# A prefetch hint for the branch that closes the loop over the experts, on three engines

## The reference, cut to what matters

```python
logits = h @ w_router + b_router
top_val, top_idx = lax.top_k(logits, TOP_K)          # TOP_K = 4 of 32
gates = softmax(top_val)
# for every expert e, on the rows xb that chose it:
gu = xb @ w_gu[e] + b_gu[e]                           # 1024 -> 2048
x_glu, x_lin = split(gu, 2)
act = min(x_glu, 7) * sigmoid(1.702 * min(x_glu, 7)) * (clip(x_lin, -7, 7) + 1)
out = (act @ w_down[e] + b_down[e]) * gate            # 1024 -> 1024
acc[tok] += out
```

## Time and profile before

| what | value |
|---|---|
| median of three runs | 1286.19 us |
| the profiled execution's own time | 1288.51 us |
| its span, first to last instruction | 1286.3 us |
| granted TensorE clock, mean | 0.949 of full speed |
| TensorE matmuls busy | 88% of the span |
| VectorE, ScalarE busy | 32%, 15% |
| traffic of the DMA queues | 454.88 MB, mean 354 GB/s |
| chain of work that ended last | TensorE 67%, DMA 20%, VectorE 4%, issue 4% |

### The profile page before, as it was taken

One profiled execution on the slowest core, in us unless ns is written; L12 is line 12 of the kernel. 1 busy time (PEld: TensorE's weight loads), 2 busy tenths in 40 slices (PEclk: granted clock), 3 DMA queues, 4 the chain that ended last, 5 costly groups with the idle time before them and its releaser, 6 DMA issues.

```text
span 1286.3 us, 20674 instructions
## 1 busy us (share of the span) xinstructions
PE 1132.5 (88%) x6676; PEld 496.9 (39%) x6677; DVE 417.8 (32%) x1283; ACT 195.4 (15%) x419; POOL 43.9 (3%) x27
## 2 busy tenths in 40 slices
PE   4999998967877788799999998999999989869997
PEld 0667664643332222244333443443333333214432
DVE  2133735342333323312522224223332233331233
ACT  2323242141100000001111011010111011001110
POOL 0141101010000000000000000000000000000000
PEclk9998999986998999899999989999999999989898
DMA  9963229622999999999999989989999999999992
GB/s 379 347 228 141 68 85 373 258 86 109 420 421 422 422 422 422 421 422 400 410 422 422 422 323 417 423 339 421 422 423 421 422 421 423 421 423 421 405 394 106
DMA packets 76882, 454.88 MB, mean 354 GB/s; under 512 B 9868, under 2 KB 14732, under 8 KB 24524
## 3 DMA queue, kind: packets, MB, share of 16 engines
q1 hardware_dynamic: 70304, 449.76, 85.8%
q10 hardware_dynamic: 6540, 4.60, 1.3%
HBM read 451.17 MB, written 3.17 MB: 353 GB/s over the span
## 4 chain that ended last, share of the span: by engine, by line
PE 67%; DMA 20%; DVE 4%; issue 4%; ACT 2%; SPq 2%; POOL 0%; DVEq 0%; ACTq 0%
PE psum L867 24%; DMA ring<-w_gu 16%; PE psum L904 14%; PE psum L567 6%; PE psum L923 4%; PE psum L836 3%; PE psum L776 3%; PE psum L576 2%; DMA ring<-w_down 2%; SPq L481 2%; DMA ring<-w_ada 2%; PE psum L531 1%; PE psum L844 1%; PE psum L860 1%; PE psum L878 1%
## 5 line engine op out<-in xcount | busy, mean ns | idle before, releaser
L867 PE MATMUL psum<-ring,work 128*32 128x512 f32 (+2 forms) x2048 | 432.5, 621 | 34.0 <-DMA ring<-w_gu 32.5
L867 PEld LDWEIGHTS psum<-ring,work 128*32 128x32 f32 (+2 forms) x2048 | 131.6, 133 | 286.1 <-issue 196.6
L904 PE MATMUL psum<-ring,work 128*32 128x256 f32 (+2 forms) x1504 | 219.5, 480 | 18.8 <-issue 10.4
L1619 DVE SCALAR_TENSOR_TENSOR x<-psum,tiny,x 128x256 f32<-128x256 f32 (+1 forms) x512 | 155.2, 377 | 213.7 <-PE psum L923 213.7
L1588 DVE TENSOR_SCALAR work<-csb 96x128 bf16<-96x128 f32 x64 | 15.4, 280 | 403.0 <-PE psum L867 402.0
L980 ACT ACTIVATE work<-psum 128x256 f32<-128x256 f32 (+6 forms) x207 | 88.5, 443 | 345.7 <-PE psum L904 220.7
L904 PEld LDWEIGHTS psum<-ring,work 128*32 128x32 f32 (+2 forms) x1504 | 87.7, 130 | 136.4 <-issue 109.6
L1236 ACT ACTIVATE work<-work 128x128 f32<-128x128 f32 (+2 forms) x64 | 25.0, 391 | 573.2 <-DVE work L1602 573.2
L567 PE MATMUL psum<-h,ring 128*128 128x320 f32 x320 | 91.3, 443 | 1.2 <-ACT h L1015 1.2
L923 PE MATMUL psum<-work 32*128 32x320 f32 (+2 forms) x512 | 83.1, 481 | 1.4 <-ACT work L980 1.1
L567 PEld LDWEIGHTS psum<-h,ring 128*128 128x128 f32 x320 | 62.0, 195 | 26.9 <-issue 1.6
(11 more groups left out here) (209 smaller groups left out, 615.8 us busy)
## 6 DMA issues: line engine op xcount, KB each, us to landing
ring<-w_gu SPq DMA_DIRECT2D x256, 1024.0 KB, 20.6
ring<-w_down SPq DMA_DIRECT2D x128, 1024.0 KB, 18.9
ring<-w_ada SPq DMA_DIRECT2D x12, 2048.0 KB, 9.3
ring<-w_in SPq DMA_DIRECT2D x7, 2048.0 KB, 29.9
ring<-w_out SPq DMA_DIRECT2D x2, 2048.0 KB, 11.5
x<-xT SPq DMA_DIRECT2D x1, 1280.0 KB, 6.0
yT<-x SPq DMA_DIRECT2D x2, 640.0 KB, 3.9
work<-b_exp ACTq DMA_DIRECT2D x3, 384.0 KB, 16.4
```

The source lines that it names most:

```text
L867: last = mm(o, xg[:, kk, 0:m], cols(ring[:, kk, :]), start=False, stop=kk == KD - 1)
L904: last = mm(o, actT[:, kk, 0:m], ring[:, GU_UNITS + kk // 2, c1_:c1_ + n], start=False, stop=kk == 7)
L1619: last = stt(x[:, f, cols], bank[SPREAD_BANKS[u]][:, cols], mod[:, 40 + f, sq_:sq_ + 1], x[:, f, cols], ALU.mult, ALU.add)
```

## The change

The loop over the experts 1 to 30 in `passes` asks for a prefetch hint for its own closing branch, on each of the three engines that run `passes`. It is the same loop otherwise; the engine is now named explicitly since the option belongs to the general form of the loop.

```diff
             start(0, 0, 0)
             expert(0, 0, 0, True, False)
             most = eng.value_load(cmaxi[0:1, 0:1], min_val=0, max_val=T)
-            with eng.Fori(1, NE - 1) as e:
+            with nc.Fori(1, NE - 1, engines=[eng.engine], hint_back_edge=True) as e:
                 expert(e, e, 0, False, False)
             expert(NE - 1, NE - 1, 0, False, True)
             finish(NE - 1, 0)
```

## The result

The changed kernel takes 1291.78 us in the median (14 runs, 1289.36 to 1295.95) and the kernel before, in the same comparison, 1287.87 us (14 runs). The ratio is 1.0030, 95% interval 1.0016 to 1.0045: slower by 2 to 6 us. The prediction said 1287.0 us and a range up to 1290.8, with 0.89 for a change within 0.3%. It started from 1286.19 us, the median of the first three runs of the kernel before; the median of fourteen lies 1.7 us higher.

What follows compares the result with a forecast made beforehand. Weight transfers were taken to set the pace mostly, TensorE at large experts and the tail. Nothing removed plus 0.8 us added to the 1286.19 us median gave 1287.0 us, range 1284.0 to 1290.8 us.

Steps and rivals of the forecast that it cites:

- What bounds the kernel, and the fetches: Experts' loop: transfers mostly set the pace, TensorE at large experts and the tail; no code fetched, so the hint removes 0 us.
- What the change adds: Head of each loop body: one instruction on three engines, 30 times, taken at 0.16 us each, between 36 ns and 0.30 us.
- 26.4: Sign to look for: TensorE's 14 open waits ahead of L860 grow from 24.2 to about 26.4 us in total.
- Where it lies: VectorE and ScalarE hide the instruction beside waits; TensorE's 14 open edges between bodies take it, 2.2 us, but most are absorbed.
- I count five: 5 x 0.16 = 0.8 us: TensorE's edges between bodies: about five, mainly by large experts, count in full at 0.16 us each, 0.8 us in all.
- 14 x 0.30 = 4.2 us: Upper bound of the cost: all 14 open TensorE edges count, each at a register load's 0.30 us.
- (a): Loop's closing branch: the hint is dropped or costs no time, 1286.2 us; chance 0.10.
- (b): TensorE's closing branch shortens from 208 to 76 ns, 1285 us, chance 0.03; or unseen fetches vanish, 1277.6 us, chance 0.03.
- The 76 ns: Lowest of 30 records of TensorE's closing branch, median 208 ns; taken as a hinted branch's length, saving at most 0.13 us per edge.
- (c): Loop's head is fetched again though present, throwing nothing out; 1288.8 us; chance 0.05.
- (d): TensorE's code between L836 and L904: the fetched head displaces a needed block, 1.6 to 3.9 us per iteration, 1300 to 1340 us; chance 0.07.

Runs made afterwards that it cites:

- e1_plain: Against the kernel before: the loop in the general form with the engine named, no hint, same instructions; ratio 1.0013 (0.9995 to 1.0032).
- e3_act_dve_hint: Against the kernel before: the hint on ScalarE and VectorE alone, none on TensorE; ratio 1.0004 (0.9985 to 1.0023).
- e9_load_mid: Against the kernel before: no hint, one more load of the expert's count in the middle of TensorE's loop body; ratio 1.0001 (0.9981 to 1.0022).
- e5_pe_load: Against the kernel before: no hint, one more load of the expert's count at the head of TensorE's loop body; ratio 1.0030 (1.0011 to 1.0050).
- e11_late_again: Against the kernel before, second run: the hint on TensorE alone, in the middle of the body instead of at its head; ratio 1.0006 (0.9983 to 1.0028).

## Why the prediction was wrong

**What bounds the kernel, and the fetches: right.** No instruction packet in the loop before or after. The hint has nothing to bring in: the body is on the engine after its first pass. The Trainium skill ("Runtime: NRT & Kernel Launch", Instruction fetch mechanics) has only two blocks held and a taken branch beyond them fetched anew, which could have made the hint a gain. Every profile here speaks against that rule for this loop: none of the fourteen has an instruction packet between 366 and 1236 us.

**What the change adds: right in kind and size.** One record per body and engine; 0.15 us at an open edge, with the longer branches in it, against the 0.16 us assumed. The open waits grew to 26.6 us where 26.4 was said; that this is so close is owed in part to the 0.48 us ahead of expert 28.

**Where it lies: right for two engines.** VectorE and ScalarE pay nothing that can be seen, although their branches doubled in length, which was not foreseen.

**The step that failed** is the sum: "I count five: 5 x 0.16 = 0.8 us". It took a delay at an edge to cost its own length where it counts and nothing where it doesn't. The measured cost is 3.9 us by the loop (942.6 us in the mean of the four profiles with TensorE's hint at the head, 938.7 in the three without any), and about 3 us of these lie in experts 10 to 17: 252.5 us before, 255.5 after. Taken apart in the changed kernel's profile, expert 16 has 1.8 us, 1.7 of it in matmuls at the lower clock, expert 17 has 0.8 with the clock at 0.94 for 0.97, and experts 10 and 15 with the edges behind them have 0.3 each; experts 11 to 14 are even. So 1.7 of the 3.9 us are the clock's at expert 16, a term that the sum did not have. The 0.8 us of expert 17 may be the clock's too, but that isn't shown: its clock is at 0.94 without any hint at the head in e1_plain, e3_act_dve_hint and e9_load_mid as well (53.08 to 53.12 us), and experts 10 to 17 together take 252.2 to 252.5 us there. What is left, 1.4 to 2.2 us, is the length of the delays, which the sum put at 0.8, and what the clock does elsewhere; with loops of one program up to 2.5 us apart it can't be told better. The prediction read the clock in the earlier trace rows only as a column; the edge ahead of expert 16, with 1.85 us of idle between two stretches at full clock, was a place to ask what a little more would do. The upper bound of 14 x 0.30 = 4.2 us was not passed by the measured 3.9, but that is luck: its price per edge was twice the 0.15 us measured, and at that price even all 14 edges make only 2.1 us.

**The starting point.** Of the 4.8 us between 1287.0 and 1291.78, 1.7 aren't in the change's cost at all. The sum set out from the median of three runs, 1286.19 us, where fourteen have 1287.87; the cost itself was missed by 3.1 us. The measured 0.3% is just what the prediction called the least that can be told.

**The rivals.** (a) did not happen: the hint has a cost. (b) did not happen; the branch is longer. The 76 ns that it was priced by belong to the loop's last branch, at 1243.0 us, the one that falls through; no taken branch was that short. (c) did not happen: no packet. (d), the slower one, named the wrong mechanism: nothing of the body was lost. What it feared for the body happened behind the loop, once. With a hint on TensorE, two of its branches there wait for code; in the changed kernel from 1250 to 1260 us and from 1250 to 1262 us:

```profile
L441 PEldq COMPARE_BRANCH  x4: 70/142/4197, 1252.6 to 1259.3; - x4
```

```profile
L438 PEldq COMPARE_BRANCH  x4: 208/221/3123, 1252.3 to 1261.0; - x4
```

Together they take 7.3 us of the sequencer. Nearly all of it is covered, since matmuls of the last expert are queued over it. What shows is one idle time of 0.5 us behind the first of the two branches, on the chain that ended last; the kernel before has none there:

```profile
1259.04 0.82 PE L923 MATMUL psum<-work 32*128 32x320 f32 x8 [0.52 <-issue]
```

From the last expert's start to the end the kernel before takes 41.5 us and the changed one 41.0; the other profiles take 38.6 to 41.4 us, with and without a hint, so the whole stretch is too scattered to show it.

**What stays open.** What decides whether an idle time lets the clock fall: the edges ahead of experts 11 and 16 change between 1.9 and 2.0 us, yet ahead of expert 4 the kernel before has 2.2 us of idle, and experts 4 and 5 run at a granted clock of 1.00 throughout (408.64 to 468.29 us); in e5_pe_load it holds behind 2.36 and 2.37 us. No run varied the delay between the hint's 0.15 us and the load's 0.66. Where the rest of the 3.9 us comes from is open too; so is why experts 9, 14, 17 and 29 have one stretch at the lower clock in some executions and two in others, and whether a hint in the middle of the body costs 1 us.

## What to carry to other kernels

Look for instruction packets inside the loop before hinting its branch; where the trace has none, there is nothing for the hint to bring in. Here it only cost, at the head of the body, where the sequencer is already late. Where TensorE sits idle between two stretches at full clock, a delay can cost more than its length: look in the neighbouring windows what the clock does, and place added sequencer work where matmuls are queued. The same place is where something is to be gained: two loads of registers taken off the head of the body gave 0.5%.

## What the runs showed of the hardware that was not expected

A hint that is armed, that is, one that has run while its branch is still to come, makes the other compare-and-branches of its own engine longer too, not only the one it names. On ScalarE the branches of L438 went from 45 to 99 ns, on VectorE from 56 to 124 ns, on TensorE from 202 to 209 ns. It begins at the hint's place: in e11_late_again one hint stands at 923.5 us in the middle of a body, and TensorE's branches ahead of it (first row, 916 to 923.5 us) and behind it (second row, 923.6 to 940 us) are

```profile
L438 PEldq COMPARE_BRANCH  x2: 202/202/202, 917.0 to 918.6; - x2
```

```profile
L438 PEldq COMPARE_BRANCH  x6: 209/216/219, 923.6 to 936.7; - x6
```

The code behind the loop is the other point. Before 366 us q8, the queue that brought in TensorE's body, carries one packet less with the hint. Before and after:

```profile
q8 instruction: 18, 0.29, 0.3%
```

```profile
q8 instruction: 17, 0.28, 0.3%
```

Over the whole run both carry 24; the one that is lacking comes behind the loop. All seven profiles with a hint on TensorE have 17 up to 366 us, and all seven without it 18. So without the hint one packet more was there ahead of time, and with it TensorE waits: the 4.2 us begin at 1254.1 us and a packet is recorded between 1255.5 and 1256 us, the 3.1 us begin at 1261.0 and the next is recorded between 1261.5 and 1262 us. In the kernel before no branch of `by_size` behind the loop takes more than 0.42 us.
